# Queries 768 to 1023 of each mLSTM head read keys 0 to 767 through an accumulated matrix memory

## What is computed

```python
b = jnp.cumsum(fc, axis=-1)
d = jnp.where(causal, b[..., :, None] - b[..., None, :] + ic[..., None, :], -jnp.inf)
m_t = jnp.maximum(b + m[..., None], jnp.max(d, axis=-1))
s = jnp.einsum('bhtd,bhsd->bhts', qc, kc) * jnp.exp(d - m_t[..., None])
a = jnp.exp(b + m[..., None] - m_t)
num = a[..., None] * jnp.einsum('bhtd,bhdv->bhtv', qc, C) + jnp.einsum('bhts,bhsv->bhtv', s, vc)
den = a * jnp.einsum('bhtd,bhd->bht', qc, n) + jnp.sum(s, axis=-1)
h = num / jnp.maximum(jnp.abs(den), jnp.exp(-m_t))[..., None]
C_new = decay[..., None, None] * C + jnp.einsum('bhsd,bhsv->bhdv', wk, vc)
n_new = decay[..., None] * n + jnp.sum(wk, axis=2)
```

## Time and profile before

| | |
|---|---|
| runs | 3098.46, 3101.23, 3101.94 us; median 3101.23 |
| span of the profiled execution | 3099.1 us; none of the three times is marked as its own, the median is 2.1 us above the span |
| PE busy | 2993.6 us (97%), weight loads 2786.5 us |
| DVE, ACT, POOL busy | 1686.5, 866.9, 1078.5 us |
| mean granted TensorE clock | 0.989 |
| the four heads | first QT matmul at 1575.7 us, last values at 2153.8 us |

### The profile page before, as it was taken

How to read it: one execution, slowest core, us unless ns; L and a number is a source line. 1 busy time by engine, 2 the same in 40 slices (tenths; PEclk the granted TensorE clock), 3 DMA queues, 4 the chain that set the end, 5 groups by cost and what they waited for, 6 DMA issues and landing times.

```text
span 3099.1 us, 50797 instructions
## 1 busy us (share of the span) xinstructions
PE 2993.6 (97%) x19628; PEld 2786.5 (90%) x19628; DVE 1686.5 (54%) x2584; ACT 866.9 (28%) x1542; POOL 1078.5 (35%) x746
## 2 busy tenths in 40 slices
PE   7998899999999999999989999998999999999998
PEld 7885789999999998999967878787998999999997
DVE  5877445544444455444357786878226345444445
ACT  4000542222212224111144444444005122222211
POOL 3232023555555533333201011102332365555553
PEclk9999899999999999999989999999999999999999
DMA  8555211111111113333255655648410111111121
GB/s 228 139 141 141 80 50 42 42 41 54 47 54 47 55 35 119 132 103 104 89 185 193 224 198 198 238 175 294 133 43 28 55 55 41 35 46 48 54 75 57
DMA packets 278260, 319.01 MB, mean 103 GB/s; under 512 B 25909, under 2 KB 217653, under 8 KB 276898
## 3 DMA queue, kind: packets, MB, share of 16 engines
q1 hardware_dynamic: 257777, 250.82, 26.2%
q10 hardware_dynamic: 13048, 40.28, 3.4%
q0 software_dynamic: 7296, 25.96, 2.4%
HBM read 225.68 MB, written 92.19 MB: 103 GB/s over the span
## 4 chain that ended last, share of the span: by engine, by line
PE 79%; DVE 10%; ACT 4%; issue 3%; PEld 1%; DMA 1%; POOL 0%; SPq 0%; another core or an unknown queue 0%; DVEq 0%; ACTq 0%; POOLq 0%; PEldq 0%
PE ps L426 19%; PE ps L427 19%; PE ps L428 19%; PE ps L861 3%; PE ps L860 3%; PE ps L862 3%; PE ps L2404 2%; PE ps L1460 2%; PE ps L1503 1%; DVE CT L1897 1%; PE ps L1469 1%; PE ps L1470 1%; DVE RST L2061 1%; PE ps L1471 1%; DVE HT L2079 1%
## 5 line engine op out<-in xcount | busy, mean ns | idle before, releaser
L426 PE MATMUL ps<-AH,WH 128*128 128x352 f32 x3072 | 999.1, 325 | 5.0 <-POOL WL L413 2.0
L428 PE MATMUL ps<-AH,WL 128*128 128x352 f32 x3072 | 985.2, 321 | 0.0
L427 PE MATMUL ps<-AL,WH 128*128 128x352 f32 x3072 | 985.2, 321 | 0.0
L426 PEld LDWEIGHTS ps<-AH,WH 128*128 128x128 f32 x3072 | 576.7, 188 | 30.3 <-issue 23.9
L427 PEld LDWEIGHTS ps<-AL,WH 128*128 128x128 f32 x3072 | 577.8, 188 | 1.1 <-issue 0.2
L428 PEld LDWEIGHTS ps<-AH,WL 128*128 128x128 f32 x3072 | 576.9, 188 | 0.0
L411 POOL TENSOR_SCALAR WH<-RAW 128x1024 fp32r<-128x1024 f32 x152 | 180.3, 1186 | 953.0 <-PEq L433 752.6
L413 POOL TENSOR_TENSOR WL<-RAW,WH 128x1024 fp32r<-128x1024 f32 x152 | 400.7, 2636 | 12.7
L1084 DVE TENSOR_TENSOR X<-X,ps 128x352 f32<-128x352 f32 x432 | 225.2, 521 | 264.4 <-PE ps L862 134.0
L975 ACT ACTIVATE SGF<-ps 128x352 f32<-128x352 f32 x192 | 88.7, 462 | 680.0 <-PE ps L428 679.8
L1036 DVE TENSOR_TENSOR HR<-SGF 128x352 f32<-128x352 f32 x144 | 92.8, 644 | 288.4 <-ACT SGF L975 286.5
(11 more groups left out here) (355 smaller groups left out, 5097.0 us busy)
## 6 DMA issues: line engine op xcount, KB each, us to landing
RAW<-in_ffn_w SPq DMA_DIRECT2D x128, 512.0 KB, 3.8
CT<-in_state_mlstm_C SPq DMA_DIRECT2D x32, 1024.0 KB, 5.5
out_C_s<-CT SPq DMA_DIRECT2D x32, 1024.0 KB, 6.0
RAW<-in_ml_w_in SPq DMA_DIRECT2D x32, 512.0 KB, 3.9
RAW<-in_conv_w_pw SPq DMA_DIRECT2D x24, 512.0 KB, 8.1
...
```

The lines of the kernel that those rows point to most:

```text
L426: pe.matmul(ps[:, bank, 0:CW], wh[:, k, cols], hi[:, k, cs], start=(k == 0), stop=False)
L427: pe.matmul(ps[:, bank, 0:CW], wh[:, k, cols], lo[:, k, cs], start=False, stop=False)
L428: mm = pe.matmul(ps[:, bank, 0:CW], wl[:, k, cols], hi[:, k, cs], start=False, stop=(k == nk - 1))
```

## The change

- The query chunks are taken in the order 0, 3, 1, 2 (`QB`). Chunk 3 (queries 768 to 1023) has scores only against key blocks 6 and 7 (`KB0`), so that there are 2 + 2 + 4 + 6 = 14 steps.
- Keys 0 to 767 reach chunk 3 through C and n of the first six blocks. The prompt memory is cut at block `MID` = 6: ACT copies the four PSUM tiles to CM (4 copies of 128x512) before block 6 starts the banks anew, and DVE's key sums go on in a second tile, KS2. `carried(vt)` multiplies CM with the scaled queries QA: 16 exact fp32 matmuls of 256 columns, spread over two slots without a step, which start the PSUM group that values of blocks 6 and 7 then add to.
- QA: PE makes plain queries by 4 fp32 matmuls (`carried_queries`), ACT two decay rows AQ, DVE their product (128x1024).
- The denominators: PE makes n as a column by 4 narrow fp32 matmuls, ACT copies it to NCOL, DVE adds four terms (`carried_sums`).
- The outputs C and n of the whole prompt are now put together: POOL multiplies CM by a decay (128x2048) and adds it to CPO (128x2048); for n PE adds a second fp32 matmul with F2O, a tile of ones times the decay, that POOL makes.
- Slots: 16 instead of 20. `HALVES` puts the 16 halves of the sample memories in slots 2 to 14, with two halves in slots 2, 3 and 8.
- CM, QA, AQ and KS2 lie in xch(h + 1)'s buffer. So SP loads xch(h + 1) later: after the store of sample 2, behind the store of C, in front of the load of sample 5.
- The row buffers HT are taken in another order, so that chunk 3 does not wait for the store of chunk 2.

```diff
+        QB = (0, 3, 1, 2)
+        KB0 = (0, 6, 0, 0)
+        MID = 6
-        steps = [(tc, i) for tc in range(4) for i in range(2 * tc + 2)]
+        steps = [(tc, i) for tc in range(4) for i in range(KB0[tc], 2 * QB[tc] + 2)]
...
-        LAST = {0: 1, 1: 5, 2: 11, DEC: 17, END: 19}
-        SLOT0 = 2
-        IS_STEP = SLOT0 + 2 * DEC_B - 2
+        SLOTS = [0, 1, None, None] + list(range(2, NS))
+        NSLOT = len(SLOTS)
+        FINAL = {0: 1, 1: 3, 2: 7, END: 13}
+        LAST = {tc: SLOTS.index(r) for tc, r in FINAL.items()} | {DEC: 14}
+        HALVES = {2: (0, 1), 3: (2, 3), 4: (4,), 5: (5,), 6: (6,), 7: (7,), 8: (8, 9), 9: (10,), 10: (11,), 11: (12,), 12: (13,), 13: (14,), 14: (15,)}
+        IS_STEP = 13
...
-            if not last:
-                sp.wait_ge(tok_mm, 18 * h + 18)
-                sp.dma_start(xch(h + 1)[:], inner_tiles(XCS, h + 1)).then_inc(ld_xc, 16)
...
-            sp.wait_ge(cp_ev, 4 * h + 4)
-            sp.dma_start(o["C_p"][0, 0, bass.ds(h, 1)].rearrange("h (k p) v -> p (h k) v", p=P), CPO[:]).then_inc(cps_out, 16)
...
+                if b == 2:
+                    sp.wait_ge(cp_fin, FIN0 + 3 * h + 3)
+                    sp.dma_start(o["C_p"][0, 0, bass.ds(h, 1)].rearrange("h (k p) v -> p (h k) v", p=P), CPO[:]).then_inc(cps_out, 16)
+                    sp.wait_ge(psum_old, OLD0 + 4 * h + 4)
+                    if not last:
+                        sp.dma_start(xch(h + 1)[:], inner_tiles(XCS, h + 1)).then_inc(ld_xc, 16)
...
             xo_load(pool, h, 0)
+            wait(pool, sd_mm, 2 * h)
+            pool.wait_ge(ab_done, AB0 + 4)
+            pool.tensor_scalar(F2O[:], ones_1[:], AB[:, h, 2:3], 1.0, ALU.mult, ALU.mult).then_inc(cp_fin, 1)
             pool.wait_ge(dec_split, h + 1)
             vm(0)
             vm(1)
             vm(2)
+            cm = CM[(h + 1) % 2]
+            pool.wait_ge(carry_mm, CARRY0 + h + 1)
+            pool.tensor_scalar(cm[:], cm[:], AB[:, h, 2:3], 1.0, ALU.mult, ALU.mult).then_inc(cp_fin, 1)
             vm(3)
+            pool.wait_ge(cp_ev, 4 * h + 4)
+            pool.wait_ge(cp_fin, FIN0 + 3 * h + 2)
+            pool.tensor_tensor(CPO[:], CPO[:], cm[:], ALU.add).then_inc(cp_fin, 1)
             vm(4)
...
+            def carried_queries():
+                pe.wait_ge(bd_done, 2 * h + 2)
+                pe.wait_ge(qk_ev, 12 * h + 8)
+                for dt in range(VT):
+                    mm = pe.matmul(ps[:, 3 + dt // 2, dt % 2 * 256:dt % 2 * 256 + 256], BQ[:, dt], xch(h)[:, dt, TC[1][0]:TC[1][0] + 256],
+                                   start=True, stop=True)
+                mm.then_inc(qk_mm, 1)
...
+            def carried(vt):
+                if vt == 0:
+                    pe.wait_ge(num_ev, 5 * h + 1)
+                v0 = vt % 2 * 256
+                for k in range(VT):
+                    mm = pe.matmul(ps[:, vt // 2, v0:v0 + 256], CM[(h + 1) % 2][:, k, vt * P:(vt + 1) * P], QA[(h + 1) % 2][:, k],
+                                   start=(k == 0 and vt % 2 == 0), stop=False, skip_group_check=True)
+                if vt == VT - 1:
+                    mm.then_inc(carry_mm, 1)
...
             pe.wait_ge(np_ev, 9 * h + NB)
-            pe.matmul(ps[:, 4, :], ones_1[:], KS[:], start=True, stop=True)
+            for dt in range(VT):
+                mm = pe.matmul(ps[:, 7, 8 * dt:8 * dt + 8], KS[:, dt * P:(dt + 1) * P], ones_1[:, 0:8], start=True, stop=True)
+            mm.then_inc(sd_mm, 1)
+            pe.matmul(ps[:, 4, :], ones_1[:], KS2[(h + 1) % 2][:], start=True, stop=False)
+            pe.wait_ge(cp_fin, FIN0 + 3 * h + 1)
+            pe.matmul(ps[:, 4, :], F2O[:], KS[:], start=False, stop=True)
...
+            for m in range(2):
+                t = TC[1][0] + m * P
+                act.activation(AQ[(h + 1) % 2][:, m * P:(m + 1) * P], ROWB[:, t:t + P], ACT.Exp, bias=AB[:, h, m:m + 1])
             act.wait_ge(bt_done, 8 * h + 8)
-            act.activation(WS[:], BT[:, NB - 1], ACT.Exp, bias=RT[:, h, NB:]).then_inc(ws_done, 1)
+            act.activation(WS[:, 0:MID], BT[:, MID - 1, 0:MID], ACT.Exp, bias=RT[:, h, NB:NB + 1])
+            act.activation(WS[:, MID:NB], BT[:, NB - 1, MID:NB], ACT.Exp, bias=RT[:, h, NB + 1:NB + 2]).then_inc(ws_done, 1)
...
+                        act.copy(CM[(h + 1) % 2][:, dt], ps[:, dt, :]).then_inc(mid_ev, 1)
...
+            dve.wait_ge(ws_done, h + 1)
+            dve.tensor_tensor(QA[(h + 1) % 2][:], ps[:, 3:5, :].rearrange("p b (v t) -> p (b v) t", t=256),
+                              AQ[(h + 1) % 2][:].unsqueeze(1).to_broadcast([P, VT, 256]), ALU.mult).then_inc(qa_ev, 1)
...
+            def carried_sums():
+                dve.wait_ge(n_ev, N_EV0 + h + 1)
+                wait(dve, den_mm, 4 * h)
+                qa = QA[(h + 1) % 2]
+                dve.tensor_scalar(PS[:, 1], qa[:, 0], NCOL[:, 0:1], None, ALU.mult).then_inc(psum_old, 1)
+                for k in range(1, VT):
+                    dve.wait_ge(psum_old, OLD0 + 4 * h + k)
+                    dve.scalar_tensor_tensor(PS[:, 1], qa[:, k], NCOL[:, k:k + 1], PS[:, 1], ALU.mult, ALU.add).then_inc(psum_old, 1)
+            carried_sums()
```

More of the change, by code:

```diff
@@ L239, in program @@
         WKL = misc("WKL", [P, 2, DH], F32R)
[L240 removed]
+        F2O = misc("F2O", [P, P])
         QZ = misc("QZ", [P, DEC_B * (VT * NDEC + DEC_T)])
@@ L1725, in phase_b_act @@
                 act.copy(CPO[:, dt], ps[:, dt, :]).then_inc(cp_ev, 1)
+            act.wait_ge(sd_mm, 2 * h + 1)
+            act.copy(NCOL[:], ps[:, 7, 0:8 * VT:8]).then_inc(n_ev, 1)
             high(0)
             high(1)
-            for q in range(NS):
-                if q + 2 < NS:
-                    weights(q + 2)
+            for q in range(NSLOT):
+                r = SLOTS[q]
+                ahead = r is not None and r + 2 < NS
+                if ahead:
+                    weights(r + 2)
                 for tc in (0, 1, 2, END):
@@ L1941, in phase_b_dve @@
             dve.tensor_tensor(VS[32:64], V8[:], VS[0:32].bitcast(F32), ALU.subtract).then_inc(dec_split, 1)
-            for q in range(NS):
-                m = mem_slot(q)
+            def carried_sums():
[7 more added lines that the diff above has]
+            carried_sums()
+            for q in range(NSLOT):
+                r, hv = SLOTS[q], halves_at(q)
+                ahead = r is not None and r + 2 < NS
                 for tc in range(3):
```

225 lines of the change are left out of this document (145 added, 80 removed).

## The result

The changed kernel takes 3159.69 us (median of 4 runs, 3154.33 to 3161.32) against 3101.59 before (median of 4 runs, one more than in the table of the kernel before): a ratio of 1.0185, 95% interval 1.0173 to 1.0197. It is 58 us slower, where 9 us faster was forecast. The profiled execution has a span of 3158.8 us against 3099.1.

A forecast was written before the change was run, and what follows sets the result against it. PE was taken to set a head's time, with DVE close behind in the slots. Per head -9.1 + 3.0 + 0.7 + 1.2 + 1.9 = -2.3 us, four heads -9.2: span 3089.9, measured 3092.0, range 3066 to 3112.

The forecast's parts named there:

- PE's work: Slots of a head: 80.6 us less 17.9 removed plus 6.2 for carried, giving 68.9 us.
- DVE's work: Slots of a head: 74.5 us less 7.2 removed plus 1.6 for carried_sums, giving 68.9 us.
- How long the slots then last: Slot stage of a head: 76.4 us instead of 85.5, a gain of 9.1 (bounds 6.4 and 12.4).
- 7% of hand-over: Slots other than 2 and 3, where DVE leads: its 60.7 us of work multiplied by 1.07.
- I cost that at nothing: Slots: ACT loses decays and casts; busy 38.5 us of 85.5, so the loss was counted as zero.
- POOL's wide operations: Slots 4 to 6: scaling CM and adding into CPO hold up DVE, 3.0 us per head (between nothing and 6.9).
- Rival 4: Slots: DVE stands still for POOL's whole 6.9 us, +1.6 per head, +6.4 in all, 3108; chance 0.13.
- Projections and start of the memory stage: Before block 0: carried_queries +0.7 us (bounds 0.5 and 1.5), later WKL hand-over +1.2 (bounds 0 and 1.9), per head.
- End of the memory stage: Column form of n 0.98 us and second matmul for n 0.9: +1.9 per head, all on PE and uncovered.
- Rival 3: Slot 9: sample 5's load is late behind SP's queue, PE waits 4.3 us per head, 3109; chance 0.17.
- That the load of xch costs nothing: Load of xch(h + 1), issued near slot 6, needs 7.8 us before projections 40 us away: no cost.
- The stages outside the heads are untouched: Everything outside the four heads, including the end after the last values: no change counted.

The follow-up runs named there:

- best1: oneaccx with the mean product of a finished chunk (head_mean) issued a slot later on PE, DVE's sum and centring moved with it: +1.6 us over before.
- actorder: Changed kernel with two ACT copies moved: chunk 0's row ahead of the casts, IS ahead of gain: +32.3 us over before.
- fill: Changed kernel with unneeded matmuls on PE ahead of its three long waits per head (the third not in the last head): +32.8 us over before.
- light: Changed kernel with POOL's two wide operations touching 16 of 2048 columns, so the prompt's C is incomplete: +35.9 us over before.
- lightorder: Changed kernel with the edits of light and actorder together: +21.7 us over before.
- order2lightsp: actorder plus carried_sums in slot 2, AQ/QA behind first WK/WKL, POOL on 16 of 2048 columns, sample 5's load before C's store and xch: +24.4 us over before.
- oneacc: Changed kernel with ACT, DVE and POOL steps reordered, decays relative to prompt end, no wide POOL operations, C stored ahead of the slots: +6.1 us over before.
- oneaccx: oneacc with the load of xch(h + 1) queued behind sample 6's store: -1.0 us over before, ratio 0.9988 to 1.0008.
- best3: best1 with the last head's down-projection input loads queued later and head_var of chunks 0 and 1 behind values: -1.3 us over before.

## Why the prediction was wrong

**PE's work, right.** 68.9 us per head was worked out for the slots; best1, at a granted clock of 1.00 (head 0), shows 68.76. **DVE's work, right** to 1 us: 68.9 against 69.9 in the same stage. In the kernel after both are hidden: PE's 76.1 is the half clock, DVE's 76.7 the lock.

**How long the slots then last, wrong: the step that failed.** I added 7% of hand-over, taken from before, to DVE's work, and got 76.4 us (79.4 with POOL's 3.0). Measured 93.6. A ratio of the old order says nothing of a new one: the new order put one of ACT's copies behind casts that wait for DVE's sums, another behind `gain`, and POOL's addition beside the statistics that PE waits for in slot 4. I had looked at each engine's amount of work and, for ACT, said "I cost that at nothing". But the question was what stands ahead of the copy that PE waits for. Two of the three waits end with a copy on ACT. In the first, what held the copy up was `carried_sums` on DVE: with the copy alone moved 2.62 us of 3.08 are left, with the sums moved too 0.18. I had given the sums a price (1.6 us) and no place. In the third it was ACT's own order, and that move is nearly all of actorder's 26 us.

**No term for the clock.** The kernel before had a granted clock of 1.00 in head 1's stages, and I took every duration as if it would stay. fill shows that about 25 of the 58 us are matmuls at the lower level behind waits of 1.8 to 4.8 us. It also explains why the rest of a head cost 6.1 us more against 3.8 forecast: PE was still slow when the next head's projections began. In heads 2 and 3 of fill, at a granted clock of 1.00, it costs 3.5 us more.

**POOL's wide operations, right mechanism, wrong size.** 3.0 us per head was taken, 6.9 was the upper bound. DVE lost 76.7 - 70.9 = 5.8 us of its own time, PE stood 4.79 us, and half clock came behind it; light gives 22 us, 5.5 per head. Rival 4 (the whole POOL operation) was nearer than the forecast. The Trainium skill, "SBUF — State Buffer", section "Who interferes with whom", holds that such a pair takes turns for whole instructions; that DVE's addition ends only 0.28 us after POOL's agrees with it. That the waiting instruction then gets the next turn does not always come out: DVE's addition had begun beside POOL's VM and did not end before the wide one behind VM, and the sixteen short additions kept it out for 7.38 us.

**Projections and start of the memory stage.** +1.2 was forecast for the hand-over; PE waits 1.18 us for WKL in heads 1 and 2, 1.53 in head 3, and 4.55 in head 0, where another wait (for VL) fell from 4.69 to 2.88. **End of the memory stage:** +1.9 forecast, +1.76 measured.

**Rival 3** did not happen, for the reason given against it: the slots drift later. It came as soon as they were repaired (lightorder, order2lightsp, oneacc). **That the load of xch costs nothing** holds only for slow slots.

**Where the forecast gain is.** In oneaccx the sum can be closed against the span before: slots of the four heads together -20.2; the rest of heads 1 to 3 together +7.0; head 0, 70.1 - 65.35 = +4.8; from the last values to the end +7.1; ahead of the heads -0.4. Together -1.7, as measured (3097.3 - 3099.1 = -1.8). The slots' gain is 5 us a head. It pays for the work added outside, where 3.8 us a head were forecast and 2.3 come in heads 1 to 3 and 4.8 in head 0, and for the end, where ACT's copy, and PE behind it, waits for chunk 2's store. The prediction had no term for the end ("The stages outside the heads are untouched"); it comes once and takes 7 us of the 20. What the slots still lose (78 to 80 us against 69 of work) lies, by PE's waits in best3, with DVE's updates (1.70 and 2.20 us), DVE's sum SQH (1.69) and the state loads (up to 3.04): in best3 a state's store takes 9.0 us to land, in the kernel before 6.0. Whether fewer bytes or a fourth buffer would lift that was not tried.

The DMA view, first of the kernel before (over its whole span), then of best3:

```profile
out_C_s<-CT SPq DMA_DIRECT2D x32, 1024.0 KB, 6.0
```

```profile
out_C_s<-CT SPq DMA_DIRECT2D x32, 1024.0 KB, 9.0
```
